# Layer norms in a two-block transformer kernel: row sums kept by the residual adds, squared deviations on ScalarE, centring written into the residual

## The reference

```python
def layer_norm(x, g, b):
    xf = x.astype(jnp.float32)
    mu = jnp.mean(xf, axis=-1, keepdims=True)
    var = jnp.mean(jnp.square(xf - mu), axis=-1, keepdims=True)
    y = (xf - mu) * lax.rsqrt(var + LN_EPS)
    return (y * g + b).astype(x.dtype)

def post_norm(x, sub, g, b):
    return layer_norm(DN_ALPHA * x + sub, g, b)
# ...
h = post_norm(h, 0.5 * swiglu(h, ...), ln_g[layer, 0], ln_b[layer, 0])
h = post_norm(h, mix, ln_g[layer, 1], ln_b[layer, 1])
h = post_norm(h, 0.5 * swiglu(h, ...), ln_g[layer, 2], ln_b[layer, 2])
```

## Time and profile before

| what | value |
|---|---|
| runs before (median, lowest, highest) | 1491.96, 1490.63, 1492.5 us |
| the profiled execution | 1491.49 us, of which span 1489.8 us |
| TensorE busy | 1466.8 us, 98% of the span |
| TensorE weight loads | 1237.6 us, 83% |
| VectorE busy | 869.6 us, 58% |
| ScalarE busy | 686.1 us, 46% |
| GpSimd busy | 185.8 us, 12% |
| loads from HBM | 184 GB/s over the span |
| TensorE's granted clock, mean | 0.999 of full speed |

### The profile page before, as it was taken

The page is one execution under the profiler, slowest core; times in us unless marked ns, Lnnn a source line. Parts: engine busy times, 40 slices in busy tenths (PEclk is TensorE's granted clock), DMA queues, the critical chain, the costliest instruction groups (busy, mean ns, idle before and its releaser), DMA issues.

```text
span 1489.8 us, 20432 instructions
## 1 busy us (share of the span) xinstructions
PE 1466.8 (98%) x7688; PEld 1237.6 (83%) x7688; DVE 869.6 (58%) x1032; ACT 686.1 (46%) x851; POOL 185.8 (12%) x191
## 2 busy tenths in 40 slices
PE   9999998999999999999999999999999999999997
PEld 7988896888878888889988888888888897788886
DVE  5765756554555455657665545675455677654555
ACT  5346456444344434454434444464434378444342
POOL 1073122000010000300030000300000335500000
PEclk9999999999999999999999999999999999999999
DMA  8754554865556555465566555576556450475551
GB/s 274 238 168 160 193 171 138 273 195 183 186 175 204 188 179 196 165 208 192 180 207 216 194 185 186 174 241 201 186 181 197 139 179 30 144 223 190 177 196 57
DMA packets 198875, 274.47 MB, mean 184 GB/s; under 512 B 9632, under 2 KB 158240, under 8 KB 198560
## 3 DMA queue, kind: packets, MB, share of 16 engines
q1 hardware_dynamic: 194304, 256.62, 53.6%
q0 software_dynamic: 4368, 16.78, 3.2%
q10 hardware_dynamic: 144, 0.26, 0.0%
HBM read 272.32 MB, written 1.31 MB: 184 GB/s over the span
## 4 chain that ended last, share of the span: by engine, by line
PE 88%; DVE 5%; ACT 2%; POOL 2%; issue 1%; DMA 0%; SPq 0%; DVEq 0%; POOLq 0%; ACTq 0%
PE ps L634 25%; PE ps L636 25%; PE ps L635 25%; PE ps L746 3%; PE ps L729 3%; PE ps L740 3%; PE ps L1062 1%; PE ps L675 1%; ACT whi L1420 1%; DVE wlo L1978 1%; DVE tmp L2075 1%; DMA raw<-in_w_in 0%; PE ps L1134 0%; DVE stats L2061 0%; PE ps L1259 0%
## 5 line engine op out<-in xcount | busy, mean ns | idle before, releaser
L1978 DVE TENSOR_TENSOR wlo<-raw,whi 128x2048 fp32r<-128x2048 f32 (+1 forms) x230 | 526.6, 2292 | 319.1 <-ACT whi L1420 318.2
L1420 ACT CAST whi<-raw 128x2048 fp32r<-128x2048 f32 (+1 forms) x240 | 454.6, 1896 | 230.3 <-PE ps L636 196.0
L634 PE MATMUL ps<-whi,st_hi 128*128 128x512 f32 (+1 forms) x1064 | 419.6, 394 | 1.6 <-DVE wlo L1978 1.6
L636 PE MATMUL ps<-whi,st_lo 128*128 128x512 f32 (+1 forms) x1064 | 413.2, 388 | 0.0
L635 PE MATMUL ps<-wlo,st_hi 128*128 128x512 f32 (+1 forms) x1064 | 412.7, 388 | 0.0
L636 PEld LDWEIGHTS ps<-whi,st_lo 128*128 128x128 f32 (+1 forms) x1064 | 198.8, 187 | 42.0
L634 PEld LDWEIGHTS ps<-whi,st_hi 128*128 128x128 f32 (+1 forms) x1064 | 199.0, 187 | 41.2 <-DVE wlo L1978 2.1
L635 PEld LDWEIGHTS ps<-wlo,st_hi 128*128 128x128 f32 (+1 forms) x1064 | 199.1, 187 | 39.0
L634 PE MATMUL ps<-whi,hid_hi 128*128 128x512 f32 x400 | 156.1, 390 | 0.0
L636 PE MATMUL ps<-whi,hid_lo 128*128 128x512 f32 x400 | 155.8, 390 | 0.0
L635 PE MATMUL ps<-wlo,hid_hi 128*128 128x512 f32 x400 | 155.6, 389 | 0.0
(11 more groups left out here) (260 smaller groups left out, 1464.3 us busy)
## 6 DMA issues: line engine op xcount, KB each, us to landing
raw<-in_ffn_w SPq DMA_DIRECT2D x264, 512.0 KB, 4.3
raw<-in_w_gate_up SPq DMA_DIRECT2D x44, 512.0 KB, 4.7
raw<-in_w_in SPq DMA_DIRECT2D x32, 512.0 KB, 4.9
raw<-in_sgu_w_in SPq DMA_DIRECT2D x32, 512.0 KB, 4.7
raw<-in_w_down SPq DMA_DIRECT2D x22, 512.0 KB, 4.0
raw<-in_sgu_w_out SPq DMA_DIRECT2D x16, 512.0 KB, 4.8
raw<-in_kv_w SPq DMA_DIRECT2D x12, 512.0 KB, 4.2
raw<-in_w_proj_attn SPq DMA_DIRECT2D x8, 512.0 KB, 4.8
```

The source lines that it names most:

```text
L634: pe.matmul(o, a[0], b[0], start=start, stop=False)
L636: return pe.matmul(o, a[1], b[0], start=False, stop=stop)
L1420: act.copy(whi[:, s, 0:n], raw[:, s, 0:n]).then_inc(whi_ready, 1)
L1978: dve.tensor_tensor(wlo[:, s, 0:n], raw[:, s, 0:n], whi[:, s, 0:n].bitcast(F32), ALU.subtract).then_inc(wlo_ready, 1)
```

## The change

The sum of each row half is accumulated by the add of the residual itself. From two such sums one instruction on VectorE forms minus the mean (`mean`). ScalarE squares tmp minus the mean over the whole row with an accumulator (`deviation`), and GpSimd turns that sum into rstd with two instructions (`dev_root`). VectorE centres from tmp into res and scales res in place. The order of VectorE's statements changes: behind a SwiGLU the add of y(1, 0) stands between the centring and the scaling of block 0, and both centrings of block 1 stand before its first scaling. The norm inside the gated unit ("zv") keeps its statistics.

```diff
@@ -523,7 +530,8 @@
-        VAR = {key: i for i, key in enumerate(VAR_ORDER)}
+        VAR = {("zv", tb): tb for tb in range(2)}
+        LN = {key: i for i, key in enumerate(key for key in VAR_ORDER if key[0] != "zv")}
@@ -1456,6 +1464,13 @@
+            def deviation(n, tb):
+
+                i = LN[n, tb]
+                act.wait_ge(mean_ready, i + 1)
+                act.activation(deviations[:, tb, :], tmp[:, tb, :], ACT.Square, bias=ln_negmean[:, i:i + 1],
+                               accum_out=ln_dev[:, i:i + 1]).then_inc(dev_ready, 1)
+
@@ -1742,8 +1757,10 @@
             warm_up(ACT.Gelu)
+            deviation(("ffn", 1), 0)
             upto(last + 2)
             st_out("ln0", 0)
+            deviation(("ffn", 1), 1)
             upto(last + 3)
             st_out("ln0", 1)
@@ -1784,10 +1801,13 @@
-            swiglu(2, "ln1")
+            deviation("sgu", 0)
+            swiglu(2, "ln1", lambda: deviation("sgu", 1))
             last = first["v2"] - 1
+            deviation(("ffn", 2), 0)
             upto(last + 2)
             st_out("ln2", 0)
+            deviation(("ffn", 2), 1)
             upto(last + 3)
             st_out("ln2", 1)
@@ -1865,7 +1885,9 @@
             swiglu(3, beside=cmp_gelus, copied=keys_copied)
+            deviation(("ffn", 3), 0)
             beside(first["k2"])
+            deviation(("ffn", 3), 1)
             st_out("ln3", 0, k0=8)
@@ -1955,7 +1977,10 @@
-            swiglu(4, "ln4")
+            deviation("nsa", 0)
+            swiglu(4, "ln4", lambda: deviation("nsa", 1))
+            for tb in range(2):
+                deviation(("ffn", 4), tb)
@@ -2051,72 +2076,65 @@
                 dve.scalar_tensor_tensor(tmp[:, tb, 512 * h:512 * h + 512], res[:, tb, 512 * h:512 * h + 512], f * ALPHA,
-                                         bank(key), ALU.mult, ALU.add).then_inc(*is_read(key))
...
+                                         bank(key), ALU.mult, ALU.add,
+                                         accum_out=ln_sum[:, i, h:h + 1]).then_inc(*is_read(key))
+
+            def mean(n, tb):
+
+                i = LN[n, tb]
+                for h in range(2):
+                    dve.wait_ge(*read(("y", n, tb, h)))
+                if i == 0:
+                    dve.wait_ge(zeros_ready, 1)
+                dve.scalar_tensor_tensor(ln_negmean[:, i:i + 1], ln_sum[:, i, 0:1], ln_sum[:, i, 1:2],
+                                         minus_per_d[:, :], ALU.add, ALU.mult).then_inc(mean_ready, 1)
+
+            def centre(n, tb, h):
+
+                i = LN[n, tb]
+                if h == 0:
+                    dve.wait_ge(mean_ready, i + 1)
+                    for r in range(2):
+                        dve.wait_ge(gb_loaded[r], (GB0, GB1)[r][n])
+                t, r = (x[:, tb, 512 * h:512 * h + 512] for x in (tmp, res))
+                link(dve.scalar_tensor_tensor(r, t, ln_negmean[:, i:i + 1], gb[:, 0, 512 * h:512 * h + 512], ALU.add,
+                                              ALU.mult))
+
+            def scale(n, tb, h):
+
+                r = res[:, tb, 512 * h:512 * h + 512]
+                dve.scalar_tensor_tensor(r, r, root(n, tb), gb[:, 1, 512 * h:512 * h + 512], ALU.mult,
+                                         ALU.add).then_inc(res_ready, 1)
 
             def post_norm_ln(n, name, halved, early=False):
 
...
                 if not early:
-                    sum_out(n, 0, 0, halved)
-                sum_out(n, 0, 1, halved)
-                variance(n, 0, 2, eps)
-                norm_out(n, 0)
+                    add_out(n, 0, 0, halved)
+                add_out(n, 0, 1, halved)
+                mean(n, 0)
+                centre(n, 0, 0)
+                centre(n, 0, 1)
+                if not early:
+                    add_out(n, 1, 0, halved)
+                scale(n, 0, 0)
+                scale(n, 0, 1)
                 if name == "ln2":
...
                     st_out(name, 0, part=0)
+                add_out(n, 1, 1, halved)
+                mean(n, 1)
+                if name == "ln2":
                     st_out(name, 0, part=1)
...
+                elif name is not None:
                     st_out(name, 0, part=0)
...
+                centre(n, 1, 0)
+                centre(n, 1, 1)
+                if name not in (None, "ln2"):
+                    st_out(name, 0, part=1)
+                scale(n, 1, 0)
+                scale(n, 1, 1)
                 if name is not None:
                     st_out(name, 1)
@@ -2716,6 +2734,16 @@
+            def dev_root(n, tb):
+
+                c = RS[n, tb]
+                i = LN[n, tb]
+                eps = EPS2 if n in ("sgu", "nsa") else 4.0 * EPS2
+                pool.wait_ge(dev_ready, i + 1)
+                link(pool.tensor_scalar(meansq[:, c:c + 1], ln_dev[:, i:i + 1], 1.0 / D, eps, ALU.mult, ALU.add))
+                pool.tensor_tensor(rstd[:, c:c + 1], meansq[:, c:c + 1], minus_half[:, :],
+                                   ALU.pow).then_inc(rstd_ready, 1)
+
@@ -2738,6 +2766,7 @@
             pool.memset(upad[:, :, 0:16], 0.0)
+            pool.memset(minus_per_d[:, :], -1.0 / D)
             pool.memset(minus_half[:, :], -0.5).then_inc(zeros_ready, 1)
@@ -2826,9 +2855,9 @@
                 split(unit)
-                var_root(n, 0)
+                dev_root(n, 0)
                 split(unit + 1)
-                var_root(n, 1)
+                dev_root(n, 1)
                 norm_done(n)
```

More of the change, by code:

```diff
@@ L108, in build @@
         mv = sb("mv", [P, 2, 2])
+        ln_sum = sb("ln_sum", [P, 12, 2])
+        ln_negmean = sb("ln_negmean", [P, 12])
+        ln_dev = sb("ln_dev", [P, 12])
+        minus_per_d = sb("minus_per_d", [P, 1])
         meansq = sb("meansq", [P, 48])
@@ L190, in build @@
         squares = carve(13312, 4, 512)
+        deviations = carve(4096, 2, D)
         tmpf = tmp[:, :, :].rearrange("p a b -> p (a b)")
@@ L222, in build @@
         var_ready = sem("var_ready")
+        mean_ready = sem("mean_ready")
+        dev_ready = sem("dev_ready")
         rstd_ready = sem("rstd_ready")
@@ L2053, in add_out @@
                 key = ("y", n, tb, h)
+                i = LN[n, tb]
                 dve.wait_ge(*full(key))
                 dve.scalar_tensor_tensor(tmp[:, tb, 512 * h:512 * h + 512], res[:, tb, 512 * h:512 * h + 512], f * ALPHA,
-                                         bank(key), ALU.mult, ALU.add).then_inc(*is_read(key))
-            def stats_out(n, tb, h):
-                dve.wait_ge(*read(("y", n, tb, h)))
-                link(dve.bn_stats(stats[:, tb, 6 * h:6 * h + 6], tmp[:, tb, 512 * h:512 * h + 512]))
@@ L2093, in post_norm_ln @@
+            def scale(n, tb, h):
+                r = res[:, tb, 512 * h:512 * h + 512]
+                dve.scalar_tensor_tensor(r, r, root(n, tb), gb[:, 1, 512 * h:512 * h + 512], ALU.mult,
+                                         ALU.add).then_inc(res_ready, 1)
             def post_norm_ln(n, name, halved, early=False):
-                eps = EPS2 * (4.0 if halved else 1.0)
                 if not early:
-                    sum_out(n, 0, 0, halved)
-                sum_out(n, 0, 1, halved)
@@ L2099, in post_norm_ln @@
-                variance(n, 0, 2, eps)
-                norm_out(n, 0)
+                    add_out(n, 0, 0, halved)
[7 more added lines that the diff above has]
+                scale(n, 0, 1)
                 if name == "ln2":
-                    add_out(n, 1, 0, halved)
                     st_out(name, 0, part=0)
-                    stats_out(n, 1, 0)
+                add_out(n, 1, 1, halved)
@@ L2105, in post_norm_ln @@
+                mean(n, 1)
+                if name == "ln2":
                     st_out(name, 0, part=1)
[L2106 to L2113, removed]
-                    st_out(name, 0, part=0)
-                variance(n, 1, 2, eps)
@@ L2116, in post_norm_ln @@
[L2116 to L2119, removed]
+                elif name is not None:
+                    st_out(name, 0, part=0)
+                centre(n, 1, 0)
[4 more added lines that the diff above has]
+                scale(n, 1, 1)
                 if name is not None:
@@ L2488, in _ @@
             for tb in range(2):
-                sum_out("sgu", tb, 0, False)
+                add_out("sgu", tb, 0, False)
             upto(first["ffn", 2])
@@ L2678, in _ @@
             for tb in range(2):
-                sum_out("nsa", tb, 0, False)
+                add_out("nsa", tb, 0, False)
             upto(first["ffn", 4])
@@ L2892, in _ @@
             for tb in range(2):
-                var_root(("ffn", 4), tb)
+                dev_root(("ffn", 4), tb)
 _MATRICES = ["x", "mem", "norm_mix_pre", "norm_mem_kv", "norm_mem_pre", "norm_ffn_pre", "norm_mix_post", "w_in", "pool_w", "w_proj_pool", "w_proj_attn", "rel_bias_table",
```

## The result

| what | before | after |
|---|---|---|
| median of the runs | 1491.55 us (4 runs) | 1526.76 us (4 runs, 1524.81 to 1526.9) |
| the profiled execution | 1491.49 us, span 1489.8 | 1526.67 us, span 1524.9 |
| TensorE's granted clock, mean | 0.999 | 0.987 |

The ratio is 1.0232, with an interval of 1.0219 to 1.0244: slower, as forecast, but by 35.2 us where the sum had 14.0, and above the range of 1499 to 1509. Rival 1 gave 1507.1 and rival 4 gave 1511; neither reaches it.

The account below looks back on a forecast made before the run. TensorE, busy nearly all the span, was taken as the bound. Terms 4.3 + 4.05 + 1.9 + 2.0 + 2.0 - 0.3 = +14.0 us on 1491.49 gave 1505.5, as a median 1506.0; range 1499 to 1509.

Parts of the forecast that it names:

- Rival 1: SwiGLU norms: GpSimd's split gets in first, both scalings wait; +15.1 us in all, 1507.1; chance 0.15.
- rival 4: TensorE's clock falls to 1.2 GHz behind 3.7 us stalls at two norms; +19 us in all, 1511; chance 0.08.
- The step that failed: "sgu" and "nsa": the longer root starts scaling 0.3 us later, +0.1 us on TensorE, inside the 2.0.
- the held mean of block 1: "sgu" and "nsa": GpSimd's second split holds this mean, so st_out and TensorE's transpose come later; +2.0 us each.
- Who gets in first: SwiGLU norms: scale 0 runs first, the split next, scale 1 waits; +4.3, +4.05 and +1.9 us; chance 0.53.
- Rival 5: Not slower: the split comes behind both scalings because ScalarE's square delays a cast; 0.0 us, 1492; chance 0.05.
- Rival 2: SwiGLU norms: VectorE keeps the port for both scalings; +2.9, +2.2 and +0.2 us there, 1501; chance 0.07.
- TensorE's clock: A fall to 1.2 GHz for some 5 us, at two norms, costing half of that each time; chance 0.08.
- The mean is held: The 128x1 mean, with two SBUF tensors, waits for GpSimd's split despite its size; included in the sum.
- Rival 3: Means are free: "sgu" and "nsa" lose only 0.9 us each; +11.8 us in all, 1503.8; chance 0.12.
- Costed at nothing: Removed statistics worth nothing but in the tail; accumulator reads 0 to 0.08 us each, hidden; table loads in idle time.
- The tail: ("ffn", 4), behind the last matmul, without splits: scaling starts at 1485.55 instead of 1485.88; -0.3 us.

Follow-up runs that it names:

- e6: The changed kernel with 22, 32, 22, 7 and 32 idle identity matmuls in TensorE's five long waits; 1516.91 us, ratio 1.0169.
- e2: The changed kernel with ScalarE's square of block 0 at "sgu" and "nsa" ahead of the last cast instead of behind it; 1512.45 us, ratio 1.0135.
- e8: The kernel before, with only the add of y(1, 0) moved ahead of the scalings of block 0 in the SwiGLU norms; 1509.18 us, ratio 1.0116.
- e3: The changed kernel with the add of y(1, 0) back behind the scalings and the square ahead of one cast; 1500.62 us, ratio 1.0047.
- e5: e3 with the mean formed by a tensor_scalar instead of a scalar_tensor_tensor; 1493.52 us, ratio 1.0011.
- e7: e5 with the first scaling of block 1 ahead of its second centring, as before the change; 1492.60 us, ratio 1.0002.
- e1: The changed kernel with the add of y(1, 0) put back behind both scalings of block 0; 1511.53 us, ratio 1.0133.
- e4: The changed kernel with 30, 44, 30, 9 and 44 idle identity matmuls in TensorE's five long waits; 1524.33 us, ratio 1.0215.

## Why the prediction was wrong in size

Right were the direction and its mechanism, the order of VectorE's statements against GpSimd's splits. The 21 us that were missing come from three places. The growths of e6, at full clock, put sizes to them: the failed step 9.7 us, GpSimd's first place at most 1.1, the clock 9.6; what is left are 0.5 ahead of the norms and 0.2 in the tail.

**The step that failed: "In 'sgu' and 'nsa' scaling starts 0.3 us later."** It was worked out from durations alone, as if ScalarE took up the square when the mean was there. For the SwiGLU norms the forecast looked at what stood in ScalarE's queue around the square; for these two it did not. The diff shows the loop over `beside(first["sgo"] + k)` in the place ahead of deviation("sgu", 0), and its last cast waits for a slot that TensorE frees late. The scaling started 4.0 us late, 779.85 less the 775.85 at which the centrings ended, and that set it against the split. Cost at full clock: 6.84 and 6.90 us against 2.0 and 2.0, 9.7 us too few. The forecast's own term for these norms, the held mean of block 1, did not arise in after, since everything ran behind the split; once the square was moved up it arose as described, 1.69 and 1.81 us in e2 against 2.0.

**Who gets in first.** The forecast had the first scaling 0.06 us ahead of the split, and took that for the likeliest. The split came on the forecast's time (625.81 - 1.23 = 624.58); the add came 0.07 us later than worked out from the modelled end of its matmul (625.21 - 1.23 = 623.98, not 623.91), the same in e8 (624.37 - 0.39 = 623.98). The split won by 0.01 us, at all three SwiGLU norms. A margin of 0.06 us on modelled ends is no basis for 0.53 against 0.15. It cost little: 4.60, 4.59 and 2.17 us at full clock against 4.3, 4.05 and 1.9, that is 1.1 us. This is rival 1, whose own sum had 1.1 us as well. Which of the two wins where they start together, and why, wasn't tried on its own. Rival 5 (the split late) falls with these rows. Rival 2 (the port kept for both scalings) stays untested: it needs a split issued during the first of two scalings, and none of the traces has one.

**TensorE's clock** had 0.08, two norms and 5 us. The runs give 8.9 us in the five stretches with waits (e6), one fall elsewhere among them. Two of these waits were not in the forecast (the failed step), and at ("ffn", 3) the fall came behind 1.69 us of waiting. The forecast had seen one fall, at the end, where the clock stayed at 1.00 for some 5 us behind the last matmul, and a stall of 3.7 us is shorter than that. At ("ffn", 1) of after it stayed for only some 2 us of the wait: one case was no measure of how soon it falls. What one fall costs was set too high, 2.5 us against 1.5 to 1.7. The Trainium skill, TensorE: Matmul & The Clock Gate, "HAM oscillation — how this bites in real kernels", warns of such gaps between bursts of matmuls. The trace agrees at the four long waits (5.13 to 7.32 us), with a window at 0.50 at each (from 628 and 784 above, from 976 and 1326 at the other two); the gaps that the section describes are longer than the 1.69 us at ("ffn", 3), where the clock fell too, and there the measurement decides.

**The mean is held**: right. Rival 3 falls: 0.45 us in block 0 of "sgu", ending with the first split (773.83 + 0.45 = 774.28 against 769.62 + 4.63 = 774.25), and up to 3.18 in e3. The Trainium skill, SBUF — State Buffer, "Who interferes with whom", has a VectorE instruction with two SBUF inputs contend with a GpSimd instruction that reads SBUF, and sets no size for it; the rows of 128x1 agree. The same section lets an instruction with at most one SBUF input, outside the 2-port modes, pass; the tensor_scalar of e5, whose second operand is a pointer into SBUF, passes as well, at 0.214 us beside running splits.

**Costed at nothing, and right**: the removed statistics (e7: no difference), the accumulator reads (0.08 us, with the successor starting beside them), the table (no load for Square behind Gelu). **The tail**: -0.1 against -0.3; with the add back in its place it gains 0.7 to 0.8 (e1, e3, e5, e7), so the moved add took most of the gain there too. The square took 1.15 us where 1.06 stood in the sum.

## What to carry to other kernels

An instruction put on another engine inherits that engine's queue: before costing its duration, read what stands ahead of it there at that place and what that waits for. Where two engines exclude each other, a moved statement costs the other's whole instruction, not its own; if the margin is under the error of modelled ends, take the loss as likely as not. And a stall of TensorE of a few microseconds is to be priced with what its clock costs behind it, here 1.5 to 1.7 us for each.

## What was not expected of the hardware

The clock can fall behind waits that another execution passes unharmed. Code ahead of the change, the same in both kernels, waited 1.18 us for VectorE in before and 1.17 in after. The rows of TensorE and the windows around them, before and after:

```profile
255.71 0.66 PE L675 MATMUL ps<-con,tmp 128*128 128x128 f32 x4 [1.18 <-DVE tmp L2020]
```
```profile
254.00:256.00 2.00, 0.82 (x5) 0.39 (x5) 1.10 (x2) 1.16 (x1) 1.28 (x3) 1.00 0.56 121
256.00:258.00 2.00, 1.70 (x10) 1.17 (x9) 1.01 (x2) 0.59 (x1) 1.38 (x3) 1.00 0.99 385
```
```profile
255.82 1.11 PE L683 MATMUL ps<-con,tmp 128*128 128x128 f32 x4 [1.17 <-DVE tmp L2045]
```
```profile
254.00:256.00 2.00, 0.83 (x3) 0.39 (x4) 0.98 (x2) 1.28 (x1) 1.38 (x3) 0.92 0.49 106
256.00:258.00 2.00, 2.00 (x7) 1.39 (x8) 0.84 (x2) 0.59 (x1) 1.27 (x3) 0.50 0.98 395
```

TensorE's busy time before the fall is the same to 0.01 us, the wait is the same, and the clock is 1.00 in one and 0.50 in the other. That is most of the 1.23 us ahead of ("ffn", 1): VectorE's scaling just before it starts 0.12 us later than in before (255.02 against 254.90), its second st_lo behind it 1.23 us later (260.61 against 259.38). Such falls, at this place or in the windows from 1240, 1256 or 1264, are in the profiled executions of after, e2, e3, e4, e5, e7 and e8 and not in those of e1 and e6. What tips it stays open; a single execution's time carries a microsecond or so of it, so the small differences of e5 and e7 rest on ten and eleven executions.

Two smaller things: at four of the five norms a split that starts together with a waiting scaling takes 4.48 or 4.49 us, less than the 4.63 of one alone (4.60 at the fifth), and in e1 to e3 one that starts 0.2 to 0.3 us before the end of a scaling takes 4.68 to 4.74. And a float32 product of 128x128 with the identity shows as two rows of TensorE, 0.112 us apart (44 rows for 22 products in e6).
